# Hybrid decoder block: eight of ten input projection steps, in place of two, by seven block products each

## The reference

```python
h = rms_norm(x, norm_mix_g)
proj = h @ w_in                          # 256x1024 @ 1024x5120
qa, ka, va, qb, kb, vb, ga, gb = split(proj)   # six of 512 columns, two of 1024
qa, ka = rope(qa), rope(ka)
ya = diff_attention(qa, ka, va) @ w_da_out       # 4 heads, softmax - lam * softmax
yb = stick_breaking(qb, kb, vb) @ w_sb_out       # 8 heads
x = x + (sigmoid(ga) * ya + sigmoid(gb) * yb) @ w_o
h = rms_norm(x, norm_ffn_g)
y = moe(h)                               # top 4 of 32 experts, clamped SwiGLU, 1024 wide
out = rms_norm(x + y, norm_final_g)
```

## Time and profile before

| | before |
|---|---|
| median of 3 runs | 1124.85 us (1124.01 to 1125.22) |
| profiled execution | 1124.24 us, span 1122.5 us |
| TensorE busy (matmul) | 1066.8 us, 95% |
| VectorE busy | 222.9 us, 20% |
| ScalarE busy | 126.1 us, 11% |
| GpSimd busy | 20.0 us, 2% |
| HBM read | 436.28 MB, mean 390 GB/s |
| chain that ended last | PE 58%, DMA 40%, ACT 1% |

### The profile page before, as it was taken

The page is one execution under the profiler, slowest core; times in us unless marked ns, Lnnn a source line. Parts: engine busy times, 40 slices in busy tenths (PEclk is TensorE's granted clock), DMA queues, the critical chain, the costliest instruction groups (busy, mean ns, idle before and its releaser), DMA issues.

```text
span 1122.5 us, 11859 instructions
## 1 busy us (share of the span) xinstructions
PE 1066.8 (95%) x5057; PEld 504.1 (45%) x5057; DVE 222.9 (20%) x507; ACT 126.1 (11%) x226; POOL 20.0 (2%) x21
## 2 busy tenths in 40 slices
PE   9999999999999999999999898989898989999886
PEld 8888887634343443344334332433243324343322
DVE  5442223321112030203112110020203020202021
ACT  1201340210010001000100010000000100010002
POOL 2300000000000000000000000000000000000000
PEclk9999999999999999999999999999999999999999
DMA  8975256599999999999999999999999999999995
GB/s 339 391 307 225 85 216 281 197 403 429 434 431 431 429 431 430 433 430 433 432 433 431 430 433 431 433 430 433 433 432 431 430 433 431 433 426 426 429 427 241
DMA packets 26654, 438.16 MB, mean 390 GB/s; under 512 B 4992, under 2 KB 6272, under 8 KB 8576
## 3 DMA queue, kind: packets, MB, share of 16 engines
q1 hardware_dynamic: 26480, 437.67, 92.1%
q10 hardware_dynamic: 144, 0.07, 0.0%
HBM read 436.28 MB, written 1.05 MB: 390 GB/s over the span
## 4 chain that ended last, share of the span: by engine, by line
PE 58%; DMA 40%; ACT 1%; issue 0%; DVE 0%; another core or an unknown queue 0%; SPq 0%; ACTq 0%; DVEq 0%
DMA ring<-in_experts 40%; PE ps L1593 24%; PE ps L1639 9%; PE ps L1226 9%; PE ps L1402 2%; PE ps L1241 2%; PE ps L1507 2%; PE ps L1648 2%; PE ps L1276 1%; PE ps L1450 1%; PE ps L1447 1%; PE ps L1628 1%; PE ps L1516 1%; ACT region_va L708 0%; PE ps L1526 0%; DMA ring<-in_first 0%
## 5 line engine op out<-in xcount | busy, mean ns | idle before, releaser
L1593 PE MATMUL ps<-ring,xT 128*64 128x512 f32 x2048 | 462.8, 607 | 24.1 <-DMA ring<-in_experts 24.1
L1593 PEld LDWEIGHTS ps<-ring,xT 128*64 128x64 f32 x2048 | 145.0, 139 | 315.8 <-issue 283.6
L1639 PE MATMUL ps<-ring,region_va 128*64 128x512 f32 x1024 | 228.3, 596 | 22.9 <-ACT region_va L708 12.3
L1639 PEld LDWEIGHTS ps<-ring,region_va 128*64 128x64 f32 x1024 | 73.3, 137 | 156.4 <-issue 125.8
L1226 PE MATMUL ps<-ring 128*128 128x256 f32 x448 | 98.7, 380 | 0.0
L1226 PEld LDWEIGHTS ps<-ring 128*128 128x128 f32 x448 | 84.5, 190 | 11.8 <-issue 0.2
L1125 DVE TENSOR_SCALAR g<-ps 128x1024 f32<-128x1024 f32 x16 | 19.6, 1224 | 348.5 <-PE ps L1593 348.5
L1507 PEld LDWEIGHTS ps<-sel,x 128*128 128x128 f32 x480 | 55.4, 192 | 9.5 <-issue 9.5
L1648 PE MATMUL ps<-g,g_T 128*128 128x512 f32 x128 | 59.2, 605 | 0.0
L1147 DVE TENSOR_SCALAR region_va<-ps 128x512 f32<-128x512 f32 x32 | 22.1, 691 | 184.4 <-PE ps L1593 184.4
L1072 DVE TENSOR_TENSOR xT<-ps,g_ffn 128x512 f32<-128x512 f32 x30 | 20.7, 691 | 190.9 <-PE ps L1507 190.9
(11 more groups left out here) (218 smaller groups left out, 476.8 us busy)
## 6 DMA issues: line engine op xcount, KB each, us to landing
ring<-in_experts SPq DMA_DIRECT2D x71, 4096.0 KB, 46.2
ring<-in_experts SPq DMA_DIRECT2D x43, 2048.0 KB, 46.2
ring<-in_head SPq DMA_DIRECT2D x13, 2048.0 KB, 13.3
ring<-in_experts SPq DMA_DIRECT2D x14, 1024.0 KB, 8.5
ring<-in_first SPq DMA_DIRECT2D x7, 384.0 KB, 6.4
x<-in_x SPq DMA_DIRECT2D x2, 512.0 KB, 24.0
out<-x SPq DMA_DIRECT2D x4, 256.0 KB, 2.3
ring<-in_norm_final_g SPq DMA_DIRECT2D x1, 512.0 KB, 11.5
```

Source lines behind the costliest of these rows:

```text
L1593: last = mm(bank(banks + half)[rows, :], xT[:, 2 * m + c, rows], w[:, c, k, half * W512:(half + 1) * W512], start=False, stop=m == 3 and c ...
L1639: last = mm(bank(first + half)[rows, :], hTm[:, 2 * m + c, rows], w[:, c, k, half * W512:(half + 1) * W512], start=m == 0 and c == 0, stop ...
```

## The change

`project_by_seven` becomes the one `project` for eight steps (`SEVEN`: VB, QA, KA, VA, GA0, GA1, GB0, GB1). For VB and VA the activations stay the stationary operand and the weights stream, 256 columns. For the other six the weights are stationary, in 128x128 tiles, and 128 tokens stream, so that features end up on partitions: 2 pieces x 4 chunks per block product, 56 products of 128 columns per step. All results now end up in SBUF in pieces (`result`), by two copies of ScalarE and five adds of VectorE per step, and rotation and gate sigmoids read them from there. All block sums are made on VectorE, two of them a step ahead (`block_sums`) and two behind the sixth product (`later_sums`); a sum now takes `b_sum3 = b_sum2 - b11`. Slot 0 holds the sums for the whole stage, so the head's loads use slots 1 to 7 by the table `HEAD_SLOT`. The attention pieces are set between block products by `after_first`, `after_fourth`, `after_sixth`.

```diff
-HEAD_RING = 8
+HEAD_SLOT = {1: 1, 2: 2, 3: 3, 4: 4, 5: 5, 6: 6, 7: 7, 8: 1, 9: 2, 10: 3, 11: 5, 12: 4, 13: 6}
+HEAD_BEFORE = {8: KB, 9: VB, 10: QA, 11: VA, 12: KA, 13: GA0}
+HEAD_ORDER = (1, 2, 3, 5, 6, 7, 4, 8, 9, 10, 12, 11, 13)
+SEVEN = [VB, QA, KA, VA, GA0, GA1, GB0, GB1]
+def seven_banks(k):
+    return 0, 3 if k % 2 else 1, 2
-SLOT_OF = [6, 7, 0, 8, 1, 9, 2, 3, 10, 4, 5, 11]
+SLOT_OF = [7, 1, 8, 0, 2, 9, 3, 5, 10, 4, 6, 11]
...
-            for n in (1, 2, 3, 5, 6, 7, 4, 9, 10, 11, 12, 8, 13):
+            for n in HEAD_ORDER:
...
-            slot_free = {6: (step_done, GA0 + 1), 7: (step_done, GA1 + 1), 8: (da_read, HEADS), 9: (tro, 1),
-                         0: (step_done, GB0 + 1), 1: (step_done, GB1 + 1), 2: (yb_done, 4), 3: (ya_done, 4),
-                         10: (mix_ready, 4), 4: (wo_done, 2), 5: (wo_done, 4), 11: (wo_done, 4)}
+            slot_free = {7: (step_done, GA1 + 1), 1: (step_done, GB0 + 1), 8: (da_read, HEADS), 0: (step_done, GB1 + 1),
+                         2: (step_done, GB1 + 1), 9: (tro, 1), 3: (yb_done, 4), 5: (ya_done, 4),
+                         10: (mix_ready, 4), 4: (wo_done, 2), 6: (wo_done, 4), 11: (wo_done, 4)}
...
@@ ScalarE @@
             stick_shares(0)
+            seven_copies(1)
             stick_turned(0)
+            seven_copies(2)
             stick_out(0)
-            seven_copies(1, VA, va3, 2)
+            seven_copies(3)
             stick_shares(1)
+            seven_copies(4)
+            seven_copies(5)
+            sigmoid_of(GA0)
             stick_turned(1)
-            sigmoid_of(GA1, sga, 1)
             stick_out(1)
+            seven_copies(6)
+            sigmoid_of(GA1)
...
@@ VectorE @@
+            def block_sums(k):
+                i = SEVEN[k]
+                (b11, b12), (b21, b22) = blocks_of(i)
+                dve.wait_ge(slot_loaded[HEAD_SLOT[i]], 16 * head_turn(i))
+                nc.vector.tensor_tensor(b12, b12, b11, ALU.subtract).then_inc(b_sums, 1)
+                if k:
+                    dve.wait_ge(seven_done, 6 * k - 4)
+                dve.wait_ge(b_sums, 4 * k + 1)
+                nc.vector.tensor_tensor(b_sum2, b22, b12, ALU.subtract).then_inc(b_sums, 1)
+            def later_sums(k):
+                (b11, b12), (b21, b22) = blocks_of(SEVEN[k])
+                if k:
+                    dve.wait_ge(seven_done, 6 * k)
+                dve.wait_ge(b_sums, 4 * k + 2)
+                nc.vector.tensor_tensor(b_sum3, b_sum2, b11, ALU.subtract).then_inc(b_sums, 1)
+                nc.vector.tensor_tensor(b_sum4, b21, b_sum2, ALU.subtract).then_inc(b_sums, 1)
...
+            add_second(6)
             diff_max(range(0, 4))
-            diff_weights((0, 1))
+            add_fourth(6)
+            block_sums(7)
+            add_fifth(6)
+            diff_weights((0,))
+            add_sixth(6)
+            later_sums(7)
+            add_last(6)
             diff_max(range(4, 8))
-            diff_weights((2, 3))
+            add_second(7)
+            diff_weights((1,))
+            add_fourth(7)
+            diff_weights((2,))
+            add_fifth(7)
+            add_sixth(7)
+            diff_weights((3,))
+            add_last(7)
...
@@ TensorE @@
+                def product(g, a, b, start):
+                    if i in (VB, VA):
+                        for c in range(4):
+                            last = mm(seven_bank(k, g).rearrange("p f t -> p (f t)"), a[:, c, :], b[:, c, :],
+                                      start=start and c == 0, stop=c == 3, skip_group_check=True)
+                        return last
+                    for f in range(2):
+                        for c in range(4):
+                            last = mm(seven_bank(k, g)[:, f, :], b[:, c, f * P:(f + 1) * P], a[:, c, :],
+                                      start=start and f == 0 and c == 0, stop=c == 3, skip_group_check=True)
                     return last
...
-            project(QA)
+            project(1)
             stick_turn(0)
-            project(KA)
+            project(2)
             stick_values(0)
-            project_by_seven(1, VA)
-            pe.wait_ge(sb_ev, 1)
-            stick_scores(1)
-            project(GA0)
-            stick_turn(1)
-            project(GA1)
+            project(3, after_fourth=second_scores)
+            project(4)
+            project(5, after_fourth=lambda: stick_turn(1))
             stick_values(1)
...
-            project(GB0, halfway=lambda: diff_scores(0))
-            diff_scores(1)
+            project(6, after_first=lambda: diff_scores(0), after_sixth=lambda: diff_scores(1))
...
-            project(GB1, halfway=first_weights)
+            project(7, after_fourth=first_weights)
```

More of the change, by code:

```diff
@@ L228, in build, with result @@
         va3 = r_va[:, :].rearrange("p (a n) -> p a n", a=NT)
+        step_out = {VB: vb3, VA: va3, QA: qaT, KA: kaT, GA0: sga[:, 0:4, :], GA1: sga[:, 4:8, :], GB0: sgb[:, 0:4, :],
+                    GB1: sgb[:, 4:8, :]}
+        def result(i, tokens, features):
+            if i in (VB, VA):
+                return step_out[i][:, tokens, features * T:(features + 1) * T].rearrange("p (f t) -> p f t", f=2)
+            return step_out[i][:, 2 * features:2 * features + 2, tokens * P:(tokens + 1) * P]
         hTm = r_va[:, :].rearrange("p (c s) -> p c s", c=KC)
@@ L627, in _ @@
             diff_exp(range(0, 4))
-            sigmoid_of(GB0, sgb, 0)
+            seven_copies(7)
             diff_exp(range(4, 8))
@@ L655, in _ @@
             nc.scalar.activation(ossq, ossq, ACT.Sqrt).then_inc(da_std, 1)
+            sigmoid_of(GB0)
+            sigmoid_of(GB1)
             act.wait_ge(tro, 1)
@@ L869, in rotate @@
-                last.then_inc(evac[i], 1)
-                dve.wait_ge(evac[i], 1)
+                    own.step(nc.vector.scalar_tensor_tensor(out=turned[:, :, w, :], in0=x4[:, :, 1 - w, :],
+                                                            scalar=(-scale, scale)[w],
+                                                            in1=sin.unsqueeze(1).to_broadcast([P, 2, T]), op0=ALU.mult,
+                                                            op1=ALU.mult))
+                own.settle()
@@ L882, in diff_max @@
+            add_fourth(4)
+            add_fifth(4)
+            stick_scan(1, range(2))
+            add_sixth(4)
+            later_sums(5)
+            add_last(4)
+            stick_scan(1, range(2, 4))
+            add_second(5)
+            stick_weights(1)
+            add_fourth(5)
+            add_fifth(5)
+            block_sums(6)
+            add_sixth(5)
+            later_sums(6)
+            add_last(5)
             def diff_max(heads):
@@ L1385, in _ @@
             wait_slot(10)
-            pe.wait_ge(evac[GB0], 1)
-            pe.wait_ge(evac[GB1], 1)
+            pe.wait_ge(seven_left, 8)
+            pe.wait_ge(seven_read, 40)
             def transpose_outputs():
@@ L1439, in out_weights @@
             def out_weights(j, half):
-                return slot((12 + half) % HEAD_RING, KC, W512)[:, j, :]
+                return slot(HEAD_SLOT[12 + half], KC, W512)[:, j, :]
             for j in range(KC):
@@ L1561, in loaded @@
                         if m % 2 == 0 and (opening or closing):
-                            before = len(range(s or HEAD_RING, HEAD_LOADS, HEAD_RING)) if s < HEAD_RING else 0
+                            before = list(HEAD_SLOT.values()).count(s)
                             pe.wait_ge(slot_loaded[s], (before + (1 if opening else 3) + q) * 16)
```

255 lines of the change are left out of this document (138 added, 117 removed).

## The result

| | before | after |
|---|---|---|
| median | 1124.86 us (4 runs, 1124.01 to 1125.22) | 1117.81 us (4 runs, 1117.69 to 1118.3) |
| profiled execution | 1124.24 us, span 1122.5 | 1118.3 us, span 1116.5 |
| QA's first product | 47.37 | 47.30 |
| output projection begins | 157.65 | 151.00 |
| first load of the stream | 227.28 | 220.63 |

The ratio is 0.9941, 95% interval 0.9929 to 0.9952: 7.05 us faster by the medians, outside the 2.2 us that a measurement can't tell from no change. The forecast was 6.1 us and 1118.7. The profiled executions differ by 5.9 (1124.24 to 1118.3), the medians by 7.05; the position of the stream's first load, which both traces show to a hundredth, differs by 6.65. That last number is the one to explain.

A forecast was written before the change was run, and what follows sets the result against it. The prediction took the DMA stream, started by the first expert product behind gapless TensorE work, as the bound. 8.9 us saved less 2.7 of waits and some tenths gave 6.1: 1118.7 us, range 1115.7 to 1122.5.

The forecast's parts named there:

- The bound and where it starts: Expert stream: DMA sets the end, its start waits for the first expert product, so the end moves one for one.
- TensorE's 8.9 us: Six projection steps on TensorE: 83.9 us removed, 75.0 added, so 8.9 us back if nothing makes it wait.
- The three waits: TensorE waits before QA's third, GA0's fourth and GB1's fourth product: 1.5, 0.8 and 0.3 us, together 2.6 to 2.7.
- "Some tenths" for breaks: Added breaks between products and scores: some tenths of a microsecond may go, taking 6.2 us gained to 6.1.
- The costless edits: GpSimd sums gone, SBUF results, gate sigmoids behind head norms (table load 1.28 us in slack), new load order: cost nothing.
- (a): Head stage: no waits, the whole 8.9 us arrives, 1116.0 us; chance 0.08.
- (b): Head stage: more waits, 5.2 us with block sums of 1.5 us and adds of 0.5, 1120 to 1123; chance 0.12.
- (d): VectorE between GA0 and GB1 becomes the bound, block sums of 1.8 us giving 9.7 us of waits, 1126; chance 0.03.
- (c): Stream start set by something other than the first expert product, so nothing reaches the end, 1124.9; chance 0.05.
- (e): Six steps: 128-column products dearer in long runs, 0.2475 us each, 13.9 us per step, 1125.5; chance 0.04.

The follow-up runs named there:

- Filling products: The changed kernel plus 24 unread bf16 products of 512 columns on TensorE between the last head values and the output projection: 1123.26 us.
- The map alone: The kernel before with only the head's loads in slots 1 to 7 and the changed order of slots: 1124.86 us, ratio 1.0001.

## Why the prediction was right

**The bound and where it starts: right.** The stream's first load moved from 227.28 to 220.63, the first expert product from 225.30 to 218.65, both by 6.65, and the end followed by 6.0 in the profiled spans. Filling products and the last column of the table show the one for one by themselves.

**TensorE's 8.9 us: right in kind, 0.7 too high.** Forecast 83.9 to 75.0. Before, the six steps took 83.8 by their starts: 13.91 each for QA, KA, GA0 and GA1, and 7.11, 7.10, 7.01 and 6.91 for the four halves. Here is QA's row in the kernel before with the one behind it; its 14.08 is modelled at the end, and so were the 14.01 that the prediction used.

```profile
47.37 14.08 PE L1226 MATMUL ps<-ring 128*128 128x256 f32 x64
61.28 1.47 PE L1295 MATMUL ps<-ident,ring 128*128 128x128 f32 x12
```

With the change a step takes 12.60 us, 75.6 for six, since a product comes every 0.225 and not every 0.223. The row of the expert stage that gave 0.223 was 16 products long. 8.2 us came back.

**The three waits: the mis-sized term.** The step "together 2.6 to 2.7 us" measured about 1.1:

| place | forecast | measured |
|---|---|---|
| QA, third block product | 1.5 | 0.9 |
| GA0, fourth | 0.8 | 0.2 |
| GB1, fourth | 0.3 | none, 0.6 to spare |

The first two were at the place named and released by the operation named, and the third did not come. All were laid out too long because the layout gave a block sum 1.26 us and an add 0.42 from start to start, as an operation takes that waits for the one before. Where the next doesn't need the last one's result it starts sooner: 1.13 behind a block sum, 0.34 behind an add. GA0's row of operations (one add, two sums, the last add, four instructions of rotation, one add) then ends 0.6 us earlier, which is the miss there. In QA the memsets come at 47.15, not behind an add that ends at 47.6.

**"Some tenths" for breaks: right in words, 0.4 short in the sum.** Outside the six steps and VA, the stretch from QA to the output projection had 14.2 us of other work (110.28 − 83.8 − 12.3). It still has: the six steps now take 77.1 us from start to start and VA 12.4, and 103.70 − 77.1 − 12.4 is 14.2. What the breaks between products, scores and transposes cost lies in the steps themselves, 77.1 − 1.1 of waits = 76.0 where the pace of 0.225 gives 75.6, and in VA's 0.1: 0.5 us. The prediction took 0.1.

So forecast was 8.9 − 2.7 − 0.1 = 6.1, and measured 8.2 − 1.1 − 0.5 = 6.6, with 6.58 in the stretch: one error of 1.6 us in favour, against two of 0.7 and 0.4. That the sum is nearer than its terms is luck.

**The costless edits: right, and one of them bears weight.** The map alone is 1.0001. The gates' last sigmoids now sit behind the head norms with a table load of 1.28 at 153.94 and end at 157.2. ScalarE's next work, on the output projection, has to wait for TensorE, so the cover named is there with 5.20 us to spare:

```profile
162.44 0.69 ACT L682 ACTIVATE ring<-ps,small 128x512 f32<-128x512 f32 x1 [5.20 <-PE ps L1520]
```

GpSimd's quiet is worth some 2.7 us in QA.

**The rivals.** (a), no waits, would have been 0.9 + 0.2 us better than the change: its mechanism is real, and three runs take part of it. (b) and (d) are one curve, and the runs with more sums trace it: the layout gave 5.2 us of waits at 1.5 us per block sum. One extra sum per step, spread over the four, is 0.3 us more on each, about 1.55 as an estimate, and cost 1.4 us over the waits of 1.1, 2.5 together: half of the forecast. Two extra are about 1.87 each and ended at 1125.5, where the prediction had 1125.7 at 1.8 and 1129.8 at 2.0. So, as an estimate, the change stops paying near 1.85 us per block sum, not 1.75. Longer sums themselves were not run: the extra work stands at one place of the step and not on all four, and that the same start-to-start error explains this difference is argued, not shown. (c), nothing reaches the end, is out by the filling products.

(e), dearer products of 128 columns, is out by KA's 112 records without a gap. The Trainium skill, page "TensorE: Matmul & The Clock Gate", section "Back-to-back issue gap", has 128 columns in a stream of load and matmul pairs at about 81 ns, where the columns alone would give some 56, 1.45 times as much. An estimate by that ratio puts them at 72% of the price of 256 columns, if those pay nothing on top. The f32 products here, with a new weight tile each time, take 0.225 us for 128 columns and 0.435 for 256: 52% of it. The measurement decides for f32 products; no run here has the page's case.

**Open.** The 0.5 us between the stretch's 6.58 and the medians' 7.05 is below what can be told. Why the head of an execution begins up to 1.5 us later in one trace than in another (QA at 47.21 and at 48.72) wasn't followed. No kernel here is without both waits and without a new one; both attempts to move the rotation made one.

## What to carry to other kernels

Before adding work to an engine with idle time, lay out its order against the consumer's: here VectorE was busy 69% of the stage, and the first extra operation per step cost 1.4 us and the second 4.6. Take start-to-start times from the trace in both forms, behind an operation that is waited for and behind one that isn't, since a layout of nine operations added the difference up to 0.6 us. And make one run that puts a known delay into the suspected chain: 5.19 us in and 5.18 us out settled the bound and gave the other runs a scale finer than their medians.

## What the runs showed of the hardware

- VectorE starts an operation that doesn't depend on the last one before the last one's recorded end: block sums of 1.22 us came 1.13 apart (44.52, 45.65, 46.78), adds of 0.42 were followed after 0.34 to 0.37. Behind a result that is waited for it was 1.26 (27.84 and 29.10 in the kernel before) to 1.32 (37.68 and 39.00 in the change).
- Four f32 scans of 385 columns take 3.50 us alone and 7.33 with GpSimd's sums beside the first two: one scan is 0.93 alone and 2.67 and 3.04 beside them. Such a sum of 1024 columns takes GpSimd 2.36 us with VectorE almost idle, 2.36 and 2.88 beside the scans, and 3.13 when it starts inside a block sum of VectorE, which keeps its 1.22.
- Two f32 products of 128 columns with their own weight tiles cost 0.450 us and one of 256 costs 0.435, both over whole steps: the shape in which features land on partitions is 3% dearer, and no more.
